# Asking for the experts' down weights on ScalarE's queue instead of SyncE's

## The reference

```python
for e in range(N_EXPERTS):            # 16
    he = jax.nn.silu(h @ w_gate[e]) * (h @ w_up[e])     # 1024 -> 512, twice
    y = y + gates[..., e:e + 1] * (he @ w_down[e])      # 512 -> 1024
```

## Time and profile before

| | before |
|---|---|
| median of 3 runs | 1467.97 us (1467.6 to 1468.96) |
| the profiled execution | 1477.25 us |
| its span, first to last instruction | 1475.3 us |
| mean granted TensorE clock | 0.895 of full speed |
| PE busy | 1230.1 us (83%) |
| ACT busy | 267.9 us (18%) |
| bytes through SP's queue q1 | 308.76 MB |
| bytes through ScalarE's queue q10 | 24.70 MB |
| experts of layer 0, first gate_up to last project_down | 519 to 805 us |
| experts of layer 1, the same | 1164 to 1438 us |

### The profile page before, as it was taken

The page is one execution under the profiler, slowest core; times in us unless marked ns, Lnnn a source line. Parts: engine busy times, 40 slices in busy tenths (PEclk is TensorE's granted clock), DMA queues, the critical chain, the costliest instruction groups (busy, mean ns, idle before and its releaser), DMA issues.

```text
span 1475.3 us, 14171 instructions
## 1 busy us (share of the span) xinstructions
PE 1230.1 (83%) x5286; PEld 573.2 (39%) x5286; DVE 462.0 (31%) x1084; ACT 267.9 (18%) x573; POOL 122.2 (8%) x107
## 2 busy tenths in 40 slices
PE   4899989888999299999797499967888499797883
PEld 1363333444654233333232446523566133232223
DVE  2311555766622401111011511467563111000013
ACT  1320101123511311111010412101343011000002
POOL 2000033710000200000000200043000100000001
PEclk9899999879899589999899699987599699898996
DMA  9521108549993499999998310023013799999942
GB/s 345 211 98 74 57 0 340 231 185 401 363 365 142 173 350 381 378 375 384 390 425 312 114 57 0 0 79 149 1 40 131 246 378 373 407 394 395 427 166 92
DMA packets 86030, 347.85 MB, mean 236 GB/s; under 512 B 5958, under 2 KB 37387, under 8 KB 63435
## 3 DMA queue, kind: packets, MB, share of 16 engines
q1 hardware_dynamic: 67056, 308.76, 54.4%
q10 hardware_dynamic: 14907, 24.70, 5.0%
q0 software_dynamic: 4000, 13.49, 2.7%
HBM read 302.89 MB, written 44.04 MB: 235 GB/s over the span
## 4 chain that ended last, share of the span: by engine, by line
PE 65%; DMA 16%; DVE 11%; ACT 3%; issue 2%; POOL 1%; ACTq 1%; SPq 0%; POOLq 0%; DVEq 0%
PE ps L876 17%; PE ps L494 11%; DMA ring<-in_exp_w_up 9%; PE ps L897 7%; PE ps L782 6%; PE ps L503 5%; PE ps L437 4%; DMA arena<-in_exp_w_up 3%; DMA ring<-in_w_mod 3%; PE ps L459 3%; PE ps L679 2%; PE ps L761 2%; PE ps L659 1%; PE ps L731 1%; DVE arena L1325 1%
## 5 line engine op out<-in xcount | busy, mean ns | idle before, releaser
L876 PE MATMUL ps<-ring,arena 128*64 128x512 f32 x1024 | 242.0, 628 | 27.8 <-DMA ring<-in_exp_w_up 27.7
L437 PE MATMUL ps<-cst,arena 128*128 128x128 f32 (+1 forms) x588 | 103.8, 309 | 93.7 <-DMA arena<-slots 37.1
L494 PE MATMUL ps<-u,ring 128*128 128x512 f32 (+1 forms) x416 | 169.3, 567 | 9.8 <-ACT u L1704 4.0
L1564 DVE TENSOR_TENSOR arena<-arena,ps 128x256 f32<-128x256 f32 x44 | 26.8, 610 | 425.7 <-ACT arena L1853 425.7
L437 PEld LDWEIGHTS ps<-cst,arena 128*128 128x128 f32 (+1 forms) x588 | 73.4, 158 | 181.4 <-issue 64.0
L876 PEld LDWEIGHTS ps<-ring,arena 128*64 128x64 f32 x1024 | 74.0, 144 | 173.9 <-issue 144.2
L494 PEld LDWEIGHTS ps<-u,ring 128*128 128x128 f32 x416 | 80.4, 195 | 96.1 <-issue 90.8
L897 PE MATMUL ps<-arena 128*64 128x512 f32 x512 | 115.4, 592 | 0.9 <-ACT arena L1857 0.9
L876 PE MATMUL ps<-arena 128*64 128x512 f32 x384 | 89.4, 620 | 14.0 <-DMA arena<-in_exp_w_up 14.0
L782 PE MATMUL ps<-u,ring 128*128 128x512 f32 (+1 forms) x256 | 83.6, 487 | 2.3 <-DVE h L1407 1.3
L503 PE MATMUL ps<-ring,u 128*128 128x256 f32 (+1 forms) x224 | 75.6, 497 | 7.3 <-DVE arena L1226 7.3
(11 more groups left out here) (283 smaller groups left out, 1202.1 us busy)
## 6 DMA issues: line engine op xcount, KB each, us to landing
ring<-in_w_mod SPq DMA_DIRECT2D x24, 2048.0 KB, 11.1
ring<-in_exp_w_gate SPq DMA_DIRECT2D x22, 2048.0 KB, 23.6
ring<-in_exp_w_up SPq DMA_DIRECT2D x22, 2048.0 KB, 27.2
arena<-in_exp_w_down SPq DMA_DIRECT2D x22, 2048.0 KB, 23.4
slots<-zeros SPq DMA_DIRECT2D x4, 6144.0 KB, 41.3
arena<-in_exp_w_gate SPq DMA_DIRECT2D x10, 2048.0 KB, 24.5
arena<-in_exp_w_up SPq DMA_DIRECT2D x10, 2048.0 KB, 29.8
u<-in_exp_w_down SPq DMA_DIRECT2D x10, 2048.0 KB, 25.8
```

The source lines that it names most:

```text
L437: return nc.tensor.transpose(dst, src, ident[0:n, 0:n])
L494: last = nc.tensor.matmul(bank[row:row + width, 0:T - c0], w[:, k, n:n + width], u[:, k, c0:T], start=(k == 0), stop=(k == KT - 1))
L876: last = nc.tensor.matmul(ps[BLOCK * half:BLOCK * half + BLOCK, 2 + b % 2, :].rearrange("p (s n) -> p s n", s=2), x_k, pair[:, :, a:a + 25 ...
```

## The change

SP still asks for gate and up of all places, and for down of places 0 to 2. Down of places 3 to 15 is asked for by ScalarE: in its loop over the blocks, right after `store_y(b)`, where b is the last block of place o - 3. `store_y(b)` waits until VectorE has copied the result of block b, which comes after `project_down(b)`, so the buffer is free. ScalarE loads the expert's number from the `order` tensor first (`value_load`), and waits once a layer for `order_ready`. There are 13 such DMAs a layer, 26 in all.

```diff
@@ ScalarE, experts(l)
+                down = exp_w_down[l].rearrange("e (h p j) n -> p e h (j n)", h=2, j=2)
                 act.sem_inc(S("x_turned", l), X_BUFFERS)
+                act.wait_ge(S("order_ready"), l + 1)
                 act.wait_ge(S("passes_ready"), l + 1)
...
+                    def load_down(b):
+
+                        o = blocks[b][0] + PAIRS
+                        if o < NE and blocks_through(l, o - PAIRS) == b + 1:
+                            r = rank_order(l)[o]
+                            e = nc.scalar.value_load(order[0:1, r:r + 1], min_val=0, max_val=NE - 1)
+                            act.dma_start(downs[o % PAIRS].rearrange("p (o h n) -> p o h n", o=1, h=2),
+                                          down[:, bass.ds(e, 1), :, :]).then_inc(S(f"down_landed{o % PAIRS}", l), 16)
...
                         if b + 3 + X_BUFFERS < nb:
                             load_x(b + 3 + X_BUFFERS)
                         store_y(b)
+                        load_down(b)
                     store_y(nb - 1)
@@ SyncE, experts(l)
                         load_gate_up(o, e)
-                        load_down(o, e)
+                        if o < PAIRS:
+                            load_down(o, e)
```

## The result

The changed kernel takes 1482.77 us, the median of 16 runs, against 1468.49 us for the kernel before on the same chip. The ratio is 1.0085 with a 95% interval of 1.0061 to 1.0109: 12.5 us slower (9 to 16), clear of noise. I had forecast 1478 us, slower by 10. The ratio leaves out three of the changed kernel's 16 runs, one of 6487.7 us that something outside the kernel held up and the two slowest others, 1493.5 and 1495.2 us, which count as slow runs; with these two it would be 1.0097, 14 us.

The account below looks back on a forecast made before the run. It took the saturated DMA engines to bound the expert stages, with PE waiting for up matrices. SP 0, ScalarE's instructions 0 and 5 us per layer summed to +10 us: 1478 us, range 1461 to 1490 us.

Parts of the forecast that it names:

- What bounds the kernel: Expert stages: DMA engines saturated by weights, PE waiting 41.7 us for up matrices; SP's 325.0 us of waits were free.
- The last byte lands when it did: Expert stages: same bytes on saturated DMA, so the last down lands at 784.2 us in layer 0, 1416.4 in layer 1.
- The turns: SP's and ScalarE's queues alternate piece by piece; a down takes 20.6 us, ScalarE's queue 32 us per light block.
- ScalarE's instructions at 0: ScalarE after its store: 1.2 us of request work fits in 3.7 us free before silu; cost 0.
- Stores and rows have cover: ScalarE's queue: late stores and rows are harmless; rows have 45 us, a store 22.5 us before VectorE needs its buffer.
- +5 us a layer: End of each expert stage: late downs or downs jumping ahead cost 5 us in layer 0 and 5 in layer 1.
- (b): End of stage, downs fall behind: costs 0 to 14.2 us in layer 0, 0 to 11.3 us in layer 1.
- Deferred just enough: Faster rival: downs held back yet in time, last gate and up 4.9 us earlier per layer; 1458 us, chance 0.18.
- Same: Rival: DMA engines bound, same bytes move, PE's waits only change line; 1468 us, chance 0.12.
- ScalarE did get stuck: Much slower rival: ScalarE's full queue makes requests wait for room, delaying silu and copies; 1493 us, chance 0.08.
- What would show it: Expert-stage signs: GB/s unchanged, up waits under 20 us, down waits 20 or more, last down up to 10 us later.

Follow-up runs that it names:

- deferred order on one queue: Against the kernel before: SP asks for everything, each down after gate and up of the next place, for all places; 1462.59 us, ratio 0.9964.
- typical profile: Second profiled execution of the changed kernel, nothing further changed, near its median; 1484.31 us.
- run with three buffers: Changed kernel with three buffers for the result rows instead of two; 1486.07 us, ratio 1.0111 against the kernel before.
- one queue in the order of need: Kernel before, SP asking for downs after the next place's gate and up: all places 1462.59 us, light places alone 1460.92 us.

## Why the prediction was right, point by point

**What bounds the kernel.** Right. SP's 325 us of waits were worth nothing, and taking them out brought nothing. The deferred order on one queue had the late up matrices earlier by moving a down behind them. "The last byte lands when it did" missed one thing: layer 1's input-projection weights were on SP's queue at 773.08 us, before ScalarE had asked for the last down of layer 0 at 779.25. From the start of the stage to its landing 104.33 MB moved in the typical profile and 102.30 in the one before; at the 382 GB/s of that stretch I estimate 5 us for the difference. And 402 GB/s was one window with rows beside the weights, not all: from 540 to 740 us the windows of the kernel before have 338 to 415, 382 on average. No term of the sum hangs on it.

**The turns.** The estimate that a down on ScalarE's queue waits for one of SP's pieces at each of its own holds on average: 774 packets stand against 798, and halving SP's pieces removes the loss with the change and does nothing without it. I had 20.6 us for a down beside a busy SP queue, and the first ones of each stage took 16 to 20 us in the typical profile; the later ones took up to 49.5 us.

**ScalarE's instructions at 0.** Nearly. The cover of 3.7 us exists only while ScalarE isn't held in `store_y`. On the chain above it isn't there: from the end of the last store request at 749.60 to the silu at 750.85 pass 1.25 us, on the path. With the five waits of the silu of this kind in layer 0 I estimate 6 us at most in that layer. It wasn't measured by itself.

**Stores and rows have cover.** This is the step that failed. I gave a store two blocks, 22.5 us, and stores took up to 44.9 us. Worse, I asked only who needs the buffer, not what stands behind the waiting copy: VectorE's product for the next hidden values stands behind it, and ScalarE's silu behind `store_y`, which waits for the same copy. PE's 26.7 us at L437 come through this, 17.7 of them in layer 0, where downs cost 3.2 us. So the term that I had put at nothing is the path by which most of the loss came. The run with three buffers shows that without it late downs cost as much. The cause, ScalarE's queue falling behind, was right; the path was not, and that both paths cost about the same I hadn't worked out.

**+5 us a layer.** The sum came out near, 10 of 12.5 us, its split did not: 9.5 us in layer 0 and 2.9 in layer 1. Both fives were a choice inside wide bounds, one too low and one too high, so that the sum is this near is in part luck. In layer 1 the late downs were as foreseen, but PE no longer waited for ups, and 26.8 us stood against 33.1. For layer 0 I had taken a third of (b)'s limit of 14.2 us, and two thirds came, through stores and not through (b)'s downs. In units of that argument, block 19 was due 744.7 us (789.72 - 4 x 11.26) in the profile before, 225.6 after the stage began, and started at 753.4 in the typical one, 235.4 after: 9.8 us late, with five blocks of PE's work to go and little for the DMA engines to do.

**The rivals.** "Deferred just enough" is what one queue in the order of need gives, 5.5 us faster and not 9.8. Two queues gave it only in layer 1 of the run with 8 KB pieces (269.6 us, where one queue in the order of need has 270.5). "Same" came true only with 8 KB pieces. ScalarE's requests were not short of room: they took 0.39 us (0.80 at most) with downs of up to 49.5 us outstanding. ScalarE did get stuck, but in front of the stores, on the copy.

**What would show it.** The waits at L897 came with 30 us against 20 or more, 26.8 of them in layer 1, where places 4 and 5 had 18.8 and not 5 to 8. Waits for up matrices went to 0, with under 20 named. Down 15 landed at 790.7 us in layer 0 of the typical profile (779.25 + 11.5), 7.6 us later after the start of its stage than in the earlier trace rows, and in layer 1 at the same distance as in the earlier trace rows, within 1 us. Both are inside what I had named. Two signs failed. The GB/s didn't stay as before (357 to 363 for 425, above). And the silu didn't always start with `gate_up` as its releaser: before it did 44 times of 44, in the typical profile 36 times. The other 8 times it came after 100.6 us of "issue", time in which the releaser isn't seen, and on the chain above that is ScalarE waiting in `store_y`. That was the sign of the path that I had left out.

## What to carry to other kernels

SP's 325 us of waits cost nothing here, because what was already queued kept the DMA share at 1.0; look at that share before you buy such a wait back. What these stages are sensitive to is the order in which things land (5.5 us for the order of need on one queue), and one queue keeps an order that two don't. Beside each other the two took turns by pieces (774 against 798), so the queue with many small ones (rows, stores, a matrix in 8 KB pieces) lagged behind the one with few large ones. When you put a big transfer on an engine's queue, count the pieces that the queue then has to get through in the time of one block, and follow every wait for its older transfers to the engines that are stopped in order behind it. Then add up the waits of the engine that sets the time, stage by stage, before and after: here that alone told layer 0's stores from layer 1's downs.

## What the runs showed of the hardware that was not expected

Splitting 2 MB requests with 16 KB pieces into 1 MB ones with 8 KB pieces changed a kernel with both queues loaded by 15 us (1482.8 to 1467.4) and the same kernel with one loaded queue by less than its measurement can tell (1468.0 against 1467.4). Two backlogged queues got equal numbers of pieces, whatever their sizes (774 and 798 packets with 16 KB on SP's side, 940 and 944 with 8 KB), so the bytes that a queue gets are a matter of the size of the other's pieces.

The changed kernel spreads wider: 25.5 us between the fastest and the slowest undisturbed run of 15, against 8.8 us over 16 runs of the kernel before and 15.5 over 25 in a later set. That the second queue is the reason isn't shown; with 8 KB pieces on two queues 12 runs spread by 14.7 us. The same requests are late by different amounts from one execution to the next (layer 0 took 287.9 us in one and 296.3 in the other), so one profile of such a kernel, here one that came out 13 us under the median, can hide the loss.
